# Gate projections issued in halves at new places in the mixer, delta norm ahead of the last gates

## The reference, cut to what matters

```python
def hybrid_mixer(h, ...):
    # one product h @ w_in, split: fox q/k/v, latents, delta q/k/v/z, and gate_logits (3 x 1024)
    fox_out = block_causal_attention(fox q, k, v, ...)          # first attention, 8 heads
    mla_out = block_causal_attention(q_full, k_full, mla_v, ...)  # second attention, 8 heads
    o = chunk_gated_delta_rule(q_dn, k_dn, v_dn, g, beta)       # triangular inverse, then a scan over 4 chunks
    o = rmsnorm(o, dn_o_norm) * silu(dn_z)
    y_fox, y_mla, y_dn = fox_out @ w_br_fox, mla_out @ w_br_mla, o @ w_br_dn
    g_fox, g_mla, g_dn = split(sigmoid(gate_logits + b_gate), 3)
    return (g_fox * y_fox + g_mla * y_mla + g_dn * y_dn) @ w_out
```

## Time and profile before

| | us |
|---|---|
| median of 3 runs | 2831.52 (2831.47 to 2831.56) |
| the profiled execution | 2834.45 |
| its span, first to last instruction | 2832.7 |
| PE busy in the span | 2706.1 |
| DVE busy | 1383.9 |
| ACT busy | 556.7 |

### The profile page before, as it was taken

The page is one execution under the profiler, slowest core; times in us unless marked ns, Lnnn a source line. Parts: engine busy times, 40 slices in busy tenths (PEclk is TensorE's granted clock), DMA queues, the critical chain, the costliest instruction groups (busy, mean ns, idle before and its releaser), DMA issues.

```text
span 2832.7 us, 48634 instructions
## 1 busy us (share of the span) xinstructions
PE 2706.1 (96%) x19874; PEld 2427.0 (86%) x19874; DVE 1383.9 (49%) x2245; ACT 556.7 (20%) x1163; POOL 8.5 (0%) x19
## 2 busy tenths in 40 slices
PE   7999999999999999999999999899997899989999
PEld 6998768988998999876988899768996599966999
DVE  5554254324555555225521555436662466625665
ACT  2111132111111111123111111232113321123211
POOL 0000000000000000000000000000000000000000
PEclk9999999999999999998999999999998999999999
DMA  6654320234555556431124565423433144441342
GB/s 247 220 201 158 111 105 16 75 129 173 219 201 209 191 192 222 149 110 47 45 90 157 205 218 197 153 101 127 179 149 136 49 149 161 168 149 34 146 179 105
DMA packets 50169, 416.00 MB, mean 147 GB/s; under 512 B 4016, under 2 KB 4272, under 8 KB 29584
## 3 DMA queue, kind: packets, MB, share of 16 engines
q1 hardware_dynamic: 49344, 409.34, 39.2%
q0 software_dynamic: 592, 3.41, 0.3%
HBM read 411.69 MB, written 1.05 MB: 146 GB/s over the span
## 4 chain that ended last, share of the span: by engine, by line
PE 91%; DVE 3%; ACT 3%; issue 2%; DVEq 1%; ACTq 1%
PE units L734 29%; PE spots L734 22%; PE units L676 20%; PE spots L991 4%; PE units L1102 2%; PE spots L706 2%; PE units L1147 1%; PE units L1240 1%; PE units L805 1%; PE spots L715 1%; ACT squares L1308 1%; ACT probabilities L1308 1%; PE spots L1181 1%; PE units L1143 1%; PE spots L905 0%
## 5 line engine op out<-in xcount | busy, mean ns | idle before, releaser
L676 PE MATMUL units<-normed,weights 128*128 128x256 f32 x2016 | 453.9, 385 | 17.9 <-ACT normed L1308 14.9
L676 PEld LDWEIGHTS units<-normed,weights 128*128 128x128 f32 x2016 | 386.7, 193 | 80.5 <-issue 12.0
L734 PE MATMUL units<-normed,weights 128*128 128x128 f32 x2176 | 275.0, 280 | 21.7 <-DVE normed L1692 15.5
L734 PEld LDWEIGHTS units<-normed,weights 128*128 128x128 f32 x2176 | 259.7, 195 | 36.3 <-DVE normed L1692 17.4
L734 PE MATMUL spots<-normed,weights 128*128 128x128 f32 x2176 | 270.4, 278 | 0.0
L734 PEld LDWEIGHTS spots<-normed,weights 128*128 128x128 f32 x2176 | 259.6, 196 | 0.0
L1308 ACT ACTIVATE mla_q_rope<-units 128x256 f32<-128x256 f32 (+1 forms) x248 | 95.3, 387 | 591.8 <-PE units L734 554.3
L1807 DVE TENSOR_TENSOR delta_new_values<-spots,mla_q_rope 128x256 f32<-128x256 f32 x116 | 49.2, 424 | 277.9 <-PE spots L734 277.9
L734 PE MATMUL units<-hidden,weights 128*128 128x128 f32 x1472 | 180.9, 276 | 0.0
L734 PE MATMUL spots<-hidden,weights 128*128 128x128 f32 x1472 | 180.1, 275 | 0.0
L734 PEld LDWEIGHTS units<-hidden,weights 128*128 128x128 f32 x1472 | 172.0, 192 | 6.7 <-issue 6.7
(11 more groups left out here) (326 smaller groups left out, 3536.3 us busy)
## 6 DMA issues: line engine op xcount, KB each, us to landing
weights<-stream SPq DMA_DIRECT2D x140, 2048.0 KB, 7.7
values_mla_qk_mla_values<-stream SPq DMA_DIRECT2D x24, 2048.0 KB, 8.4
weights<-stream SPq DMA_DIRECT2D x46, 1024.0 KB, 5.2
weights<-stream SPq DMA_DIRECT2D x16, 768.0 KB, 5.6
constants<-consts SPq DMA_DIRECT2D x1, 1094.5 KB, 8.2
residual<-x_in SPq DMA_DIRECT2D x1, 1024.0 KB, 4.9
weights<-stream SPq DMA_DIRECT2D x4, 256.0 KB, 5.0
conv_in<-ctx_in POOLq DMA_DIRECT2D x1, 1024.0 KB, 5.1
```

Of the source, the lines that this page charges most:

```text
L676: mm = pe.matmul(dst, w[:, kt * width + col:kt * width + col + P], rhs[:, kt, :], start=(kt == 0), stop=(kt == k - 1))
L734: mm = pe.matmul(dst[:, m * P:m * P + P], weights[:, m, kt, :], moving(kt), start=(first and m == 0 and kt == 0), stop=(kt == n - 1), skip ...
```

## The change

The list in `one_order()` is written anew from the second attention on. A gate is issued as two halves, `ga` and `gb` (one output block each, 8 accumulation steps), which fill the two halves of the same bank; the step `gate` is now only ACT's sigmoid. For the first two branch products `bp` is PE's part and `bv` DVE's part, at different places of the list; all others keep the one step `br`. The new list, from the first new entry:

```diff
+    fill = [one("gb4", "gate4"), one("ga5"), one("gb5", "gate5"), one("br4"), one("br5"), one("ga6"), one("gb6", "gate6"),
+            one("ga7")]
...
+            def gate_half(c, i, m):
+                u, bank = unit(c, "gate", i // 2, i % 2)
+                w = group(c, "gate", i // 2)
+                dst = lin[:, bank, :] if m else free_unit(c, u)
+                mm = product(dst[:, m * T:m * T + T], w, KD, 512, (2 * (i % 2) + m) * P, act)
+                if m:
+                    mm.then_inc(lin_ready.handle, 1)
...
-                    elif step == "gate":
-                        plain(c, "gate", i // 2, i % 2)
+                    elif step in ("ga", "gb"):
+                        gate_half(c, i, int(step == "gb"))
...
                 if i >= 2:
                     e_.wait_ge(*taken(c, unit(c, "br", (i - 2) // 2, i % 2)[0]))
+                else:
+                    e_.wait_ge(*spot_ready.at(c, SPOT[c.sec]["values", 7][0][0] + 1))
```

More of the change, by code:

```diff
@@ L150, in one_order @@
              + lin("uv", 0, 1) + one("qrot0", "conv2") + lin("dz", 0) + one("scores4", "conv3") + lin("dz", 1)
[L151 to L163, removed]
+             + one("scores5", "soft4", "ga0", "l2_0", "gb0", "turn4", "soft5", "scores6", "spread0", "ga1", "values4",
+                   "turn5", "soft6", "scores7", "natural0", "gb1", "values5", "turn6", "soft7", "decay0", "values6",
+                   "turn7", "kk0", "values7", "qk0", "gate0", "gate1")
+             + one("bp0", "bp1", "level1_0", "bv0", "bv1", "ga2") + [("level", 1)] + one("gb2", "gate2") + [("level", 2)]
+             + one("ga3") + [("level", 3)] + one("gb3", "gate3") + [("level", 4)] + one("br2") + [("level", 5)]
+             + one("br3") + [("wu", 0)] + one("ga4"))
+    fill = [one("gb4", "gate4"), one("ga5"), one("gb5", "gate5"), one("br4"), one("br5"), one("ga6"), one("gb6", "gate6"),
+            one("ga7")]
     for c in range(CHUNKS):
-        order += [("scan_v", c)] + fill[:1] + [("scan_s", c)] + fill[1:2]
-        fill = fill[2:]
-    order += fill + [("gate", 8), ("onorm", 0), ("gate", 9), ("br", 8), ("br", 9), ("gate", 10), ("gate", 11), ("br", 10), ("br", 11)]
+        order += [("scan_v", c)] + fill[2 * c] + [("scan_s", c)] + fill[2 * c + 1]
+    order += one("onorm0", "gb7", "gate7", "br6", "br7")
+    for g in (8, 10):
+        order += [("ga", g), ("gb", g), ("gate", g), ("ga", g + 1), ("gb", g + 1), ("gate", g + 1), ("br", g), ("br", g + 1)]
     return order + [("out", i) for i in range(4)]
@@ L200 @@
             "rot": 2}
-NO_SPOT = ("lin", "gate", "br", "out", "conv", "squares", "soft", "rows", "norm", "final", "early")
+NO_SPOT = ("lin", "gate", "ga", "gb", "br", "bp", "bv", "out", "conv", "squares", "soft", "rows", "norm", "final", "early")
 def spots(order):
@@ L1120, in mixer @@
                          "natural": natural, "decay": decay, "level1": level1, "wu": wu, "onorm": onorm}[step](c)
-                    elif step not in ("norm", "conv", "soft", "rows"):
+                    elif step not in ("norm", "conv", "soft", "rows", "gate", "bv"):
                         {"scores": scores, "turn": turn, "values": values, "level": level, "scan_v": scan_v,
-                         "scan_s": scan_s, "br": branch, "out": mix_out}[step](c, i)
+                         "scan_s": scan_s, "br": branch, "bp": branch, "out": mix_out}[step](c, i)
             def plain_two(c, name, part):
@@ L2099, in mixer @@
                          "spread": spread, "natural": natural, "level1": level1, "wu": wu, "onorm": onorm}[step](c)
-                    elif step in ("conv", "scores", "soft", "values", "level", "scan_v", "scan_s", "br", "out"):
+                    elif step in ("conv", "scores", "soft", "values", "level", "scan_v", "scan_s", "br", "bv", "out"):
                         {"conv": conv, "scores": scores, "soft": normalise, "values": values, "level": level, "scan_v": scan_v, "scan_s": scan_s,
-                         "br": branch, "out": mix_out}[step](c, i)
+                         "br": branch, "bv": branch, "out": mix_out}[step](c, i)
             def norm_two(c, i):
```

## The result

| us | before | changed |
|---|---|---|
| median (lowest to highest) | 2831.54 (2831.47 to 2832.74) | 2807.4 (2804.32 to 2809.96) |
| span of the profiled execution | 2832.7 | 2805.4 |

The ratio is 0.9912, with a 95% interval of 0.9898 to 0.9926: 24.1 us, or 0.9%, faster. The forecast was 2806.3 us with a range of 2799 to 2816. The changed kernel's runs spread over 5.6 us, those of before over 1.3.

The account below looks back on a forecast made before the run. PE, busy 2706.1 of 2832.7 us, bounds the kernel through idle time and clock, its work unchanged. Waits 18.2 + clock 7.8 + hand-overs 1.4 - new wait 2.2 = 25.2 us; 2831.5 - 25.2 = 2806.3 us, range 2799 to 2816.

Parts of the forecast that it names:

- The waits of the attention and of level 1: Second attention and level 1: PE's waits there go, 12.5 us and 1.1 us gained over both layers.
- rival B: Second attention: its waits reappear before `level1` or in the levels, giving 2818 us; chance 0.12.
- The delta norm: Norm moved ahead of br 6, br 7 and gate 8: waits of 4.6 us go, 3.4 us more from the clock.
- The new wait: Gate 2's half behind `level1` waits for DVE's part of br 0: 1.1 us a layer, 2.2 in all.
- the bound of 1.3: Upper bound on PE's wait at gate 2's half behind `level1`: 1.3 us at most.
- Levels and scan at nothing: Levels and scan steps: 3.45 us of cover instead of 6.9 between dependent steps is enough, costed at nothing.
- Hand-overs: PE's ends are recorded late, so each of 18 waits is understated by about 0.1 us: 1.4 us more gain.
- The clock behind `spread`: Second attention: the 6.9 us slow stretch goes with the wait, gaining 2.2 us in each layer.
- rival A: Behind `spread`: waits go but 6.9 us at 1.2 GHz stay, full of work, giving 2813 us; chance 0.20.
- The clock at `decay`: Inside and behind `decay`: slow stretch kept at 13.8 us a layer, as the change doesn't touch its matmuls over 16 rows.
- `spread` itself: Second attention: no term for `spread`'s own duration, only for its wait and the slow clock behind it.
- What was left out: Later stages: no term in the sum; slow stretches shifting with their start were allowed 3.4 us either way.

Follow-up runs that it names:

- the yardstick: The changed kernel run once more, with no edit, beside the other follow-up kernels on the same chip: 2806.08 us.
- the two repeats: The changed kernel run again with no edit, in two later groups: 2806.08 us and 2803.8 us.
- the fastest kernel: Changed kernel with gates 0 and 1 in quarters, three spread inside and between `decay`'s passes, and DVE's br 0 ahead of the third mask: 2799.64 us.

## Why the prediction was right, point by point

**The waits of the attention and of level 1** (12.5 + 1.1): right. All are gone, and no later step took them over; rival B is out.

**The delta norm** (4.6, and 3.4 for the clock): right, shown by adding it alone (8.1 us) and by taking it away (about 8.4 after the yardstick's own difference).

**The new wait** (1.1 a layer): right in place and cause, 1.36 us in size. The masks end later against `level1` than they did, 461.79 in the first layer with `level1` at 459.49, so the bound of 1.3 was just too low. Moving DVE's part of br 0 ahead of the mask removed it.

**Levels and scan at nothing**: right. Half the cover is enough everywhere; no wait in the levels or the scan.

**Hand-overs** (1.4): no run isolates them; what the other terms leave over is about 0.8 us.

**The clock behind `spread`** (4.4 expected): half right. It left the second layer at once, but in the first layer 3.4 us remained although PE did not wait; in the two repeats it is absent in three mixers of four. So the wait isn't needed for the fall, which is what rival A said; but it does not stay at 6.9 us, which is what A priced. Over all profiles in which PE doesn't wait there and a gate half follows, it came in eight mixers of sixteen, at 3.4 us each; with a quarter between the two passes of `spread`, in none of six.

**The clock at `decay`** (unchanged at 13.8): the term that was mis-sized. It measured 10.2 us in both layers of all three executions of the changed kernel, 3.4 us less, 3.4 us of gain over both layers. It was at the edge of my range for the term. The step that failed is the one from "the change doesn't touch those" matmuls to an unchanged stretch: with the half ahead of `values 5` and no wait there it is 10.2 us in nearly all profiles. What makes it is shown: the matmuls over 16 rows, run one after another. Left out, or broken up in pieces of at most 2.4 us, they leave no slow stretch.

**`spread` itself** was costed at nothing. Before, the scores' last matmuls and `spread` followed one another:

```profile
409.43 0.93 PE L878 MATMUL spots<-mla_k_rope,mla_q_rope 32*128 32x128 f32 x8
410.30 1.99 PE L938 MATMUL spots<-rows,constants 8*128 8x256 f32 x8
412.47 2.70 PE L938 MATMUL spots<-rows,constants 16*128 16x256 f32 x8 [0.17 <-ACT probabilities L1308]
```

That is 0.9 us and two passes of 1.9 at full clock, 4.7 in all beside the wait. Now the same 24 matmuls take 2.9 us, interleaved (1297.00 to 1299.92): about 1.8 us a layer of gain that I did not foresee.

**What was left out**: the stages outside the mixer stretch. 2.1 us of the gain went back there in the profiled execution; PE's slow stretches fall differently once everything starts earlier, and its waits moved by a few us. Of these I had only said that they might move. In all profiles the part behind lies between 1280.3 and 1288.1 us.

The mixer stretches can be split into PE's waits, half of the time that it worked at 1.2 GHz, and the rest:

| us, first and second layer | waits | lost to the clock | the rest |
|---|---|---|---|
| before | 9.0, 9.2 | 10.8, 10.7 | 233.1, 233.0 |
| changed | 1.4, 1.4 | 6.8, 5.1 | 230.8, 230.8 |
| gain, both layers | 15.5 | 9.5 | 4.5 |
| forecast | 16.0 | 7.8 | 1.4 |

The sum was therefore too small by 3.4 (`decay`) and 3.6 (`spread`), too large by 1.7 (`spread`'s clock), 0.5 (new wait) and some 0.6 (hand-overs): 4.2 us, the difference in the stretches. The forecast of the median came so close because 2.1 us went back outside the stretches, and because the gain, counted in a profiled execution 2.9 us above the median, was taken off the median. Neither was foreseen: the mechanism was right, the agreement to 1.1 us was luck.

## What to carry to other kernels

Where an engine is busy for 96% of the span, look at its clock as well as at its waits: here 9 us of waits in each mixer came with 24 us at half clock, and dense work moved in small pieces into both gave 34 us over the two mixers. Cut such filler to the size of the gap it covers: a half or a quarter of a product did what a whole one did, and what was saved covered another gap. When a filler's buffer is freed by an engine with long items queued, put the freeing item ahead of them.

## What the runs showed of the hardware

**Narrow matmuls lower the clock of a busy engine.** In `decay` PE never waited, yet its granted clock fell from 2.4 to 1.2 GHz in every kernel in which passes of 4.2 us, nearly all over 16 rows, ran uninterrupted, though not at each pass (eight of the twelve that stood alone). It stayed at 2.4 GHz in the one in which no run of them was longer than 2.4 us, and in the one that left them out. The fall outlasted its cause: dense work behind it ran at half speed for some us, even a gate half, at 6.29 us instead of 3.62.

**Two narrow products can run side by side.** `spread` contracts over 8 rows and over 16 rows at another place of the array, behind the scores' last matmuls over 32 rows. With nothing to wait for, all three together took 2.9 us instead of 4.7. The first matmul of `spread` started at 1297.03, between the scores' matmuls; which of the three kinds ran beside which, the records don't tell. The Trainium skill (TensorE: Matmul & The Clock Gate, Part 3: Packing small matmuls) says that matmuls on different row groups run concurrently; the trace agrees. With a quarter between the halves the overlap is lost, which is part of the price of the fastest kernel.

**Part of the scatter is the clock's.** The kernel before repeats within 1.3 us beside the first run of the change and within 3.7 in the groups; the kernels with the change scatter over 1.8 to 7.2 us. In the profiles the mixer stretches differ by 1.7 or 3.3 us from one execution to the next with the same rows and waits, by half of what their slow stretches differ (3.4 and 6.8 us).
